# Three Exp/Ln activations and two VectorE steps of a projection stage in another order

## The chip, the cores and the metric

The kernel runs on one core of one Trainium2 chip. The time is the device time of one execution in microseconds; three runs of the kernel before took 3581.80, 3582.93 and 3586.24 us (median 3582.93).

## The reference, cut to what matters

Two blocks of layers run one after the other on 1024 tokens of width 1024. The second block first normalises its input and multiplies it by one wide matrix (w_in, 27 units of 128 output features), and then uses slices of the product in three mixers. The stage of the change computes this product, and beside it the first mixer:

```python
proj = hn @ w_in[l]
(q_sb, k_sb, v_sb, z_ssd, x_ssd, b_ssd, c_ssd, dt_ssd,
 q_hg, f_hg, i_hg, g_hg) = jnp.split(proj, split_at, axis=-1)
...
xbc = jax.nn.silu(causal_depthwise_conv(jnp.concatenate([xs, bm, cm], axis=-1) * vmask, conv_w, conv_b))
...
y = y.reshape(bsz, L, SSD_W) * jax.nn.silu(z.astype(f32))
...
z = jnp.einsum('bhqd,bhkd->bhqk', q[:, :, start:end], k[:, :, :end]).astype(jnp.float32) * scale
log_keep = jnp.where(mask, jax.nn.log_sigmoid(-z), 0.0)
csum = jnp.cumsum(log_keep, axis=-1)
log_w = jax.nn.log_sigmoid(z) + (csum[..., -1:] - csum)
```

The silu of a unit is computed as y * exp(-ln(1 + exp(-y))), with three activations of one table set: Exp, Ln, Exp. The silu lines are the "gates" of the change. The last four lines are the stick-breaking attention, whose cumulative sum is made with matmuls.

## The kernel before, in words

The stage is the function projection_and_sticks. It interleaves two streams of work on all engines.

The first stream is the projection: 27 units u of 128 features, each in three pieces j = 0, 1, 2 of 352, 344 and 344 of the 1040 token columns. A piece has 24 matmuls on TensorE (8 blocks of the contraction, each as three products of upper and lower halves, L155). A unit's weights come in one transfer, are split in an upper half on ScalarE (split_hi, L137) and a lower half on VectorE (split_lo, L142), both issued in piece j = 1 of the unit before. VectorE scales each finished piece out of PSUM (evict, L2996). Units 7 to 14 are the x units: VectorE runs a convolution of four taps over the whole unit (L3072, L3074 at j = 0 of the next unit, L3078 twice at j = 1) and then a max into the tile ce (L3081). Units 15 to 22 are the silu units, with no taps and only the max (L3089). Both kinds are gated: ScalarE runs Exp (L2741), Ln (L2743) and Exp (L2747) over ce in place, VectorE multiplies by it (finish, L3011), and SyncE stores the unit. There is one ce, so the max of a unit waits until finish of the unit before is through (s_out). The semaphores of the gate are s_cm (the max is done), s_cx (the first Exp), s_cl (the Ln), s_ce (the last Exp).

The second stream is the stick-breaking attention: 56 tiles c (14 for each of 4 heads) of up to 512 columns, one tile a slot. For a tile TensorE makes the logits z in one of two banks (L2918, on the diagonal also L2921), ScalarE runs Abs, Exp and Ln (L2767, L2769, L2771), VectorE forms sp (L3112), ScalarE its upper half (L2786) and VectorE its lower half (L3121). TensorE adds the sums to the same bank (L2931, L2933), ScalarE makes the weights from it (L2777), and TensorE multiplies them with the values (L2902). A running sum acc goes along (VectorE L3101, L3103, L3117; ScalarE L2780). Slot c prepares tile c + 1 and finishes tile c.

The order is written out by hand in the function drive, the same for each engine: slot(c), and inside it, at its end, the pieces that fall into the slot. Each engine runs its instructions in that order. Pieces 15 to 59 lie in the slots (2114 to 2440 us of the trace), the rest between the phases of the third mixer's first chunks (sd.act, sd.dve, sd.pe), whose ScalarE instructions L2381, L2384, L2387 and L2391 come at the head of a phase. TensorE waits for L2387 before L2354.

Of the kernel before, what the change touches and what calls it, by code (L numbers as in the profile page):

```python
# [17 lines left out]
ACT = mybir.ActivationFunctionType  # L18
# [2473 lines left out]
def projection_and_sticks(nc, a, w, hi, lo, inv, x, x_again, x_out, over_x, heads, hg, keep, table, cst, proj, conv, o_cat, ident, ones):  # L2492
# [10 lines left out]
    NU = len(units)  # L2503
# [5 lines left out]
    gated = lambda u: is_x(u) or is_silu(u)  # L2509
    n_gated = lambda u: u - 7  # L2510
# [13 lines left out]
    with Stage(nc, "pr") as st:  # L2524
# [17 lines left out]
        ce = st.sb("ce", [P, LM])  # L2542
# [152 lines left out]
        def _(act):  # L2695
# [25 lines left out]
            def piece(p):  # L2721
                u, j = p // 3, p % 3
                if j == 0 and u - 3 in qk:
                    root(u - 3)
                if j == 1 and u + 1 < NU:
                    w.split_hi(act, (u + 1) % 2, (u + 1) // 2, free=(s_mm, 3 * (u - 1) + 3))
                if u - 2 in qk:
                    i = qk.index(u - 2)
                    if j == 0:
                        act.wait_ge(s_ev, 3 * (u - 2) + 3)  # L2730
                        wait(act, s_blk, 3 * i)
                        nc.scalar.activation(ce[:, :], ev[(u - 2) % 3][:, TAPS - 1:], ACT.Square).then_inc(s_psq, 1)
                    c0, c1 = PIECES[j]
                    act.wait_ge(s_blk, 3 * i + j + 1)
                    if j == 0:
                        wait(act, s_nrm, i - 1)
                    nc.scalar.activation(cy[i % 2][:, c0:c1], pb[:, 0:c1 - c0], ACT.Ln, bias=eps[:, :], scale=1.0 / HD).then_inc(s_pb, 1)
                if gated(u - 1) and j == 2:
                    n = n_gated(u - 1)
                    act.wait_ge(s_cm, n + 1)  # L2740
                    nc.scalar.activation(ce[:, :], ce[:, :], ACT.Exp, scale=-1.0).then_inc(s_cx, 1)  # L2741
                    act.wait_ge(s_cx, n + 1)
                    nc.scalar.activation(ce[:, :], ce[:, :], ACT.Ln, bias=1.0).then_inc(s_cl, 1)  # L2743
                if gated(u - 2) and j == 0:
                    n = n_gated(u - 2)
                    act.wait_ge(s_cl, n + 1)
                    nc.scalar.activation(ce[:, :], ce[:, :], ACT.Exp, scale=-1.0).then_inc(s_ce, 1)  # L2747
                if (u, j) == (DT + 2, 0):
                    act.wait_ge(s_sdp, 64)
                    nc.scalar.activation(par[:, 2:3], par[:, 1:2], ACT.Exp).then_inc(s_dte, 1)  # L2750
                    act.wait_ge(s_dt, 2)
                    nc.scalar.activation(tmp, tmp, ACT.Exp, scale=-1.0).then_inc(s_dte, 1)
                    act.wait_ge(s_dte, 2)
                    nc.scalar.activation(tmp, tmp, ACT.Ln, bias=1.0).then_inc(s_dte, 1)
                if (u, j) == (DT + 4, 0):
                    act.wait_ge(s_dtc, 5)
                    for name in ("ecum", "wend", "elast"):
                        nc.scalar.activation(keep[name], keep["cum" if name == "ecum" else name], ACT.Exp).then_inc(s_dtx, 1)

            def slot(c):  # L2760
# [26 lines left out]
                for p in in_slot(c):  # L2787
                    piece(p)
# [162 lines left out]
        def _(dve):  # L2951
# [56 lines left out]
            def finish(u):  # L3008
                dve.wait_ge(s_ce, n_gated(u) + 1)
                src = cy[u % 2][:, :] if is_x(u) else ev[u % 3][:, TAPS - 1:]  # L3010
                nc.vector.tensor_tensor(cy[u % 2][:, :], src, ce[:, :], ALU.mult).then_inc(s_out, 1)  # L3011

            def piece(p):
                u, j = p // 3, p % 3
                if j == 0 and u - 3 in qk:
                    i = qk.index(u - 3)
                    dve.wait_ge(s_scaled, 1)
                    dve.wait_ge(s_r, i + 1)
                    nc.vector.scalar_tensor_tensor((qn, kn)[i % 2][i // 2][:, :], ev[(u - 3) % 3][:, TAPS - 1:], gains[:, i % 2:i % 2 + 1],
                                                   cy[i % 2][:, :], ALU.mult, ALU.mult).then_inc(s_nrm, 1)  # L3020
                    dve.wait_ge(s_nrm, i + 1)
                evict(u, j)
                if j == 1 and u + 1 < NU:
                    w.split_lo(dve, (u + 1) % 2, (u + 1) // 2)
                if (u, j) == (DT + 1, 1):
                    dve.wait_ge(s_kept, 16 * KT)
                    dve.wait_ge(s_sdp, 64)
# [23 lines left out]
                if u - 2 in vs:  # L3051
                    i = vs.index(u - 2)
                    dve.wait_ge(s_vt, 3 * i + j + 1)
                    if i == 0 and j == 0:
                        dve.wait_ge(s_kept, 16 * KT)
                    if j < 2:
                        src = pb[:, :].rearrange("p (t c) -> p t c", c=P)
                        if j == 0:
                            nc.vector.tensor_copy(vt[i][0:META, 0, :], src[0:META, 0, :])
                            nc.vector.tensor_copy(vt[i][:, 1:4, :], src[:, 1:4, :]).then_inc(s_pb, 1)  # L3060
                        else:
                            nc.vector.tensor_copy(vt[i][:, 4:8, :], src).then_inc(s_pb, 1)
                    else:
                        nc.vector.tensor_copy(vt[i][:, 8, :], pb[:, 0:P]).then_inc(s_pb, 1)
                if is_x(u - 1):
                    v, n = u - 1, n_gated(u - 1)
                    src = ev[v % 3]
                    y = cy[v % 2][:, :]
                    if j == 0:
                        wait(dve, s_gone[v % 2], 16 * (n // 2))  # L3070
                        dve.wait_ge(s_ev, 3 * u)
                        nc.vector.tensor_scalar(y, src[:, 0:LM], taps[:, n, 0:1], cbias[:, n:n + 1], ALU.mult, ALU.add).then_inc(s_cc, 1)  # L3072
                        dve.wait_ge(s_cc, 4 * n + 1)
                        nc.vector.scalar_tensor_tensor(y, src[:, 1:1 + LM], taps[:, n, 1:2], y, ALU.mult, ALU.add).then_inc(s_cc, 1)  # L3074
                    if j == 1:
                        for t in (2, 3):
                            dve.wait_ge(s_cc, 4 * n + t)
                            nc.vector.scalar_tensor_tensor(y, src[:, t:t + LM], taps[:, n, t:t + 1], y, ALU.mult, ALU.add).then_inc(s_cc, 1)  # L3078
                        dve.wait_ge(s_cc, 4 * n + 4)
                        wait(dve, s_out, n)  # L3080
                        nc.vector.tensor_scalar(ce[:, :], y, LOWEST, None, ALU.max).then_inc(s_cm, 1)  # L3081
                if j == 0 and gated(u - 2):
                    finish(u - 2)
                if is_silu(u - 1) and j == 1:
                    v, n = u - 1, n_gated(u - 1)
                    wait(dve, s_gone[v % 2], 16 * (n // 2))
# [1063 lines left out]
```

## Time and profile before

| | us |
|---|---|
| profiled execution, its own time | 3581.8 |
| its span | 3580.0 |
| TensorE busy (share of the span) | 3436.8 (96%) |
| VectorE busy | 2168.6 (61%) |
| ScalarE busy | 1538.3 (43%) |
| TensorE's granted clock, mean | 0.983 |

A busy time is the sum over an engine's instructions, overlaps counted once. The granted clock is the mean over the span, as a share of 2.4 GHz. The share of the span says little about one stage; there the table of stretches and the timelines tell more. Busy times of TensorE come from modelled ends, so that its instructions overlap in a timeline.

### The profile page before, as it was taken

What the parts mean: (1) busy time and instruction counts of PE and PEld (TensorE: products, weight loads), DVE (VectorE), ACT (ScalarE), POOL (GpSimd) and SP (SyncE); (2) the same over time, 40 slices, a digit from 0 to 9 for tenths busy, and PEclk for the clock granted to TensorE, in tenths of its full rate; (3) what the DMA queues carried; (4) which work ended last, traced back from release to release, by engine and by line L of the source; (5) the groups of instructions that cost most, each with busy time, mean ns of one, the idle gap of its engine ahead of it and who ended that gap; (6) DMA issues with size and microseconds to landing.
All of it is one profiled execution on the core that took longest, in us unless ns stands there. A gap on an engine that the chain in (4) does not pass through costs nothing. (4 is left out here: it accounts for less than half of the span.)

```text
span 3580.0 us, 48153 instructions
## 1 busy us (share of the span) xinstructions
PE 3436.8 (96%) x17578; PEld 2805.4 (78%) x17578; DVE 2168.6 (61%) x4264; ACT 1538.3 (43%) x3062; POOL 121.8 (3%) x151
## 2 busy tenths in 40 slices
PE   8999999989999999999999899999879999999999
PEld 6878887867777777777777678788867877878887
DVE  5477774475555566666667637766766566644443
ACT  4254453444444454444444436664323322332222
POOL 0000001000000000000000200000000000000000
PEclk9999999999999999999999999999989999999999
DMA  4232225621111221122223411112322222222223
GB/s 148 89 110 96 89 89 175 205 74 57 54 59 56 70 68 60 61 68 71 65 67 108 164 41 35 56 64 85 123 74 94 97 84 78 104 90 98 94 94 124
DMA packets 162585, 316.84 MB, mean 89 GB/s; under 512 B 33744, under 2 KB 79360, under 8 KB 162224
## 3 DMA queue, kind: packets, MB, share of 16 engines
q1 hardware_dynamic: 144432, 268.49, 22.7%
q0 software_dynamic: 15808, 36.89, 3.3%
q10 hardware_dynamic: 2112, 8.39, 0.6%
q8 instruction: 142, 2.33, 0.3%
q14 instruction: 91, 0.75, 0.1%
HBM read 260.22 MB, written 59.71 MB: 89 GB/s over the span
## 5 line engine op out<-in xcount | busy, mean ns | idle before, releaser
L137 ACT ACTIVATE all_w_hi<-all_w_raw 128x1024 fp32r<-128x1024 f32 x241 | 253.5, 1053 | 455.2 <-PE om_z L155 261.2
L142 DVE TENSOR_TENSOR all_w_lo<-all_w_raw,all_w_hi 128x1024 fp32r<-128x1024 f32 x241 | 294.9, 1224 | 244.1 <-ACT all_w_hi L137 243.8
L155 PE MATMUL om_z<-all_hi,all_w_hi 128*128 128x512 f32 x640 | 258.4, 404 | 7.9 <-DVE all_w_lo L142 4.8
L155 PE MATMUL om_z<-all_hi,all_w_lo 128*128 128x512 f32 x640 | 257.1, 402 | 0.0
L155 PE MATMUL om_z<-all_lo,all_w_hi 128*128 128x512 f32 x640 | 254.7, 398 | 0.0
L2122 DVE CUSTOM_DVE_ANT_0 at_logit<-da_qk,at_bias 128x256 f32<-128x256 f32 (+1 forms) x384 | 130.0, 376 | 165.3 <-issue 164.7
L155 PE MATMUL pr_g<-all_hi,all_w_hi 128*128 128x344 f32 (+1 forms) x624 | 213.5, 342 | 11.8 <-PEq L45 4.9
L1668 ACT ACTIVATE at_p<-at_logit,da_pair_max 128x256 f32<-128x256 f32 (+1 forms) x384 | 177.5, 465 | 101.4 <-DVE da_pair_max L2122 101.4
L1660 ACT ACTIVATE at_pt<-da_tr 128x512 f32<-128x512 f32 (+1 forms) x192 | 101.2, 527 | 264.7 <-PE da_tr L1860 264.6
L155 PE MATMUL om_z<-om_h_hi,all_w_hi 128*128 128x512 f32 x512 | 202.4, 395 | 1.7 <-DVE all_w_lo L142 1.7
L155 PE MATMUL pr_g<-all_hi,all_w_lo 128*128 128x344 f32 (+1 forms) x624 | 202.4, 324 | 0.0
L155 PE MATMUL pr_g<-all_lo,all_w_hi 128*128 128x344 f32 (+1 forms) x624 | 201.7, 323 | 0.0
L155 PE MATMUL om_z<-om_h_lo,all_w_hi 128*128 128x512 f32 x512 | 200.0, 391 | 0.0
L155 PE MATMUL om_z<-om_h_hi,all_w_lo 128*128 128x512 f32 x512 | 199.8, 390 | 0.0
L3968 DVE TENSOR_TENSOR all_yo<-all_yo,om_z 128x512 f32<-128x512 f32 x80 | 55.0, 687 | 184.9 <-PE om_z L155 184.8
L1870 PE MATMUL da_pv<-at_v,at_pt 128*128 128x64 f32 x1280 | 164.1, 267 | 0.0
L1870 PEld LDWEIGHTS da_pv<-at_v,at_pt 128*128 128x128 f32 x1280 | 159.8, 192 | 1.9
L2139 DVE TENSOR_TENSOR da_o<-da_pv,da_rden 128x128 f32<-128x128 f32 x192 | 56.0, 292 | 167.4 <-PE da_pv L1870 161.9
L155 PEld LDWEIGHTS om_z<-all_hi,all_w_hi 128*128 128x128 f32 x640 | 122.6, 192 | 37.8 <-DVE all_w_lo L142 5.0
L3863 ACT ACTIVATE om_h_hi<-om_m 128x512 fp32r<-128x512 f32 x64 | 40.5, 632 | 255.2 <-DVE om_m L3966 255.2
L1196 ACT ACTIVATE all_w_hi<-all_w_raw 128x512 fp32r<-128x512 f32 x190 | 118.3, 623 | 72.9 <-PE da_by L1214 23.8
L155 PEld LDWEIGHTS om_z<-all_lo,all_w_hi 128*128 128x128 f32 x640 | 122.8, 192 | 28.2
(827 smaller groups left out, 8882.8 us busy)
## 6 DMA issues: line engine op xcount, KB each, us to landing
all_w_raw<-in_w_mlp SPq DMA_DIRECT2D x128, 512.0 KB, 3.5
all_w_raw<-in_w_qkv SPq DMA_DIRECT2D x136, 256.0 KB, 2.7
all_w_raw<-in_w_ug SPq DMA_DIRECT2D x48, 512.0 KB, 4.1
all_w_raw<-in_w_in SPq DMA_DIRECT2D x27, 512.0 KB, 3.5
all_w_raw<-in_w_v SPq DMA_DIRECT2D x20, 512.0 KB, 4.5
vhat<-ag_vst ACTq DMA_DIRECT2D x4, 2048.0 KB, 7.4
ow_v<-vhat SPq DMA_DIRECT2D x16, 512.0 KB, 3.3
da_before<-o_groups POOLq DMA_DIRECT2D x32, 256.0 KB, 3.8
```

Source lines behind the costliest of these rows:

```text
L137: self.nc.scalar.activation(self.hi[b][:, :], self.raw[b][:, :], ACT.Copy).then_inc(self.hi_done[b], 1)
L142: self.nc.vector.tensor_tensor(self.lo[b][:, :], self.raw[b][:, :], self.hi[b][:, :].bitcast(F32), ALU.subtract).then_inc(self.lo_done[b], 1)
L155: last = self.nc.tensor.matmul(out, wp[b][:, w], ap[:, k, cols], start=(k == 0 and m == 0), stop=(k == KT - 1 and m == 2))
L1196: self.nc.scalar.activation(self.hi[n % self.slots], self.tile[name], ACT.Copy, scale=self.scales[j] if name in ("a11", "a12") else 1.0).t ...
L1660: nc.scalar.activation(pt[t % 2][:, 0:wd], tr[:, 0:wd], ACT.Copy).then_inc(s_pt, 1)
L1668: last = nc.scalar.activation(p[t % 2][:, hh, 0:wd], logit[t % 2][:, hh, 0:wd], ACT.Exp, scale=-1.0, bias=pair_max[:, t, hh:hh + 1], accum ...
L1870: last = nc.tensor.matmul(pv[:, 64 * hh:64 * hh + 64], pt[t % 2][:, i * P:i * P + P], v[:, t + x, 64 * hh:64 * hh + 64], start=(x == 0), s ...
L2122: last = nc.vector.tensor_tensor_reduce(out=logit[t % 2][:, hh, 0:wd], in0=qk[hh][:, 0:wd], in1=bias[ag][hh][x][:, :], scale=1.0, scalar=3 ...
L2139: nc.vector.tensor_tensor(o[:, t, :].rearrange("p (h c) -> p h c", h=2), pv[:, 0:P].rearrange("p (h c) -> p h c", h=2), rden[:, t, :].rear ...
L3863: nc.scalar.activation(h_hi[:, i, :], m[n % 2][:, :], ACT.Square)
L3968: nc.vector.tensor_tensor(x[:, i, halves[h]], x[:, i, halves[h]], z[b][:, :], ALU.add).then_inc(s_ev, 1)
```

## The change

On ScalarE the first Exp of a gate goes from piece j = 2 to piece j = 1 of the following unit, and the last Exp from piece j = 0 of the unit after that to j = 2, right behind the Ln. On VectorE the split of the next unit's weights goes ahead of the eviction at j = 1, and finish goes ahead of the first taps at j = 0. No instruction is added or taken away. TensorE, GpSimd and SyncE keep their order.

```diff
@@ -2735,16 +2735,16 @@
                     if j == 0:
                         wait(act, s_nrm, i - 1)
                     nc.scalar.activation(cy[i % 2][:, c0:c1], pb[:, 0:c1 - c0], ACT.Ln, bias=eps[:, :], scale=1.0 / HD).then_inc(s_pb, 1)
-                if gated(u - 1) and j == 2:
+                if gated(u - 1):
                     n = n_gated(u - 1)
-                    act.wait_ge(s_cm, n + 1)
-                    nc.scalar.activation(ce[:, :], ce[:, :], ACT.Exp, scale=-1.0).then_inc(s_cx, 1)
-                    act.wait_ge(s_cx, n + 1)
-                    nc.scalar.activation(ce[:, :], ce[:, :], ACT.Ln, bias=1.0).then_inc(s_cl, 1)
-                if gated(u - 2) and j == 0:
-                    n = n_gated(u - 2)
-                    act.wait_ge(s_cl, n + 1)
-                    nc.scalar.activation(ce[:, :], ce[:, :], ACT.Exp, scale=-1.0).then_inc(s_ce, 1)
+                    if j == 1:
+                        act.wait_ge(s_cm, n + 1)
+                        nc.scalar.activation(ce[:, :], ce[:, :], ACT.Exp, scale=-1.0).then_inc(s_cx, 1)
+                    if j == 2:
+                        act.wait_ge(s_cx, n + 1)
+                        nc.scalar.activation(ce[:, :], ce[:, :], ACT.Ln, bias=1.0).then_inc(s_cl, 1)
+                        act.wait_ge(s_cl, n + 1)
+                        nc.scalar.activation(ce[:, :], ce[:, :], ACT.Exp, scale=-1.0).then_inc(s_ce, 1)
                 if (u, j) == (DT + 2, 0):
                     act.wait_ge(s_sdp, 64)
                     nc.scalar.activation(par[:, 2:3], par[:, 1:2], ACT.Exp).then_inc(s_dte, 1)
@@ -3012,6 +3012,8 @@
 
             def piece(p):
                 u, j = p // 3, p % 3
+                if j == 1 and u + 1 < NU:
+                    w.split_lo(dve, (u + 1) % 2, (u + 1) // 2)
                 if j == 0 and u - 3 in qk:
                     i = qk.index(u - 3)
                     dve.wait_ge(s_scaled, 1)
@@ -3020,8 +3022,6 @@
                                                    cy[i % 2][:, :], ALU.mult, ALU.mult).then_inc(s_nrm, 1)
                     dve.wait_ge(s_nrm, i + 1)
                 evict(u, j)
-                if j == 1 and u + 1 < NU:
-                    w.split_lo(dve, (u + 1) % 2, (u + 1) // 2)
                 if (u, j) == (DT + 1, 1):
                     dve.wait_ge(s_kept, 16 * KT)
                     dve.wait_ge(s_sdp, 64)
@@ -3062,6 +3062,8 @@
                             nc.vector.tensor_copy(vt[i][:, 4:8, :], src).then_inc(s_pb, 1)
                     else:
                         nc.vector.tensor_copy(vt[i][:, 8, :], pb[:, 0:P]).then_inc(s_pb, 1)
+                if j == 0 and gated(u - 2):
+                    finish(u - 2)
                 if is_x(u - 1):
                     v, n = u - 1, n_gated(u - 1)
                     src = ev[v % 3]
@@ -3079,8 +3081,6 @@
                         dve.wait_ge(s_cc, 4 * n + 4)
                         wait(dve, s_out, n)
                         nc.vector.tensor_scalar(ce[:, :], y, LOWEST, None, ALU.max).then_inc(s_cm, 1)
-                if j == 0 and gated(u - 2):
-                    finish(u - 2)
                 if is_silu(u - 1) and j == 1:
                     v, n = u - 1, n_gated(u - 1)
                     wait(dve, s_gone[v % 2], 16 * (n // 2))
```

The order of the instructions shows it at three places. First ScalarE, from the end of the slot whose piece is j = 1 of an x unit (the one at 2243 us in the trace) on. L2786 is a tile's upper half, L137 the split of the weights, L2792 and L2794 two activations on four columns, L2767 to L2771 the next tile's Abs, Exp and Ln. Before:

```order
L2786 ACTIVATE pr_sp_hi<-pr_sp 128x512
L137 ACTIVATE all_w_hi<-all_w_raw 128x1024
L2792 ACTIVATE pr_oln<-pr_oss,pr_eps 128x4
L2794 ACTIVATE pr_orr<-pr_oln 128x4
L2767 ACTIVATE pr_e<-pr_zb 128x512
L2769 ACTIVATE pr_e<-pr_e 128x512
L2771 ACTIVATE pr_e<-pr_e 128x512
L2777 ACTIVATE pr_wt<-pr_zb 128x512
L2780 ACTIVATE ox_sticks<-pr_acc 128x512
L2786 ACTIVATE pr_sp_hi<-pr_sp 128x512
L2741 ACTIVATE pr_ce<-pr_ce 128x1040
L2743 ACTIVATE pr_ce<-pr_ce 128x1040
```

And in the changed kernel, from the same place:

```order
L2786 ACTIVATE pr_sp_hi<-pr_sp 128x512
L137 ACTIVATE all_w_hi<-all_w_raw 128x1024
L2742 ACTIVATE pr_ce<-pr_ce 128x1040
L2792 ACTIVATE pr_oln<-pr_oss,pr_eps 128x4
L2794 ACTIVATE pr_orr<-pr_oln 128x4
L2767 ACTIVATE pr_e<-pr_zb 128x512
L2769 ACTIVATE pr_e<-pr_e 128x512
L2771 ACTIVATE pr_e<-pr_e 128x512
L2777 ACTIVATE pr_wt<-pr_zb 128x512
L2780 ACTIVATE ox_sticks<-pr_acc 128x512
L2786 ACTIVATE pr_sp_hi<-pr_sp 128x512
L2745 ACTIVATE pr_ce<-pr_ce 128x1040
```

The first Exp of the gate (L2742 in the changed kernel) now stands ahead of the next tile's Abs, Exp and Ln; the Ln (L2745) and the last Exp (L2747) stand behind them.

Second VectorE, at j = 0 of a unit whose two predecessors are gated (L2996 the eviction, L3011 finish, L3074 and L3076 the first taps, L3101 and L3103 the running sum of the next tile):

```order
 L2996 TENSOR_TENSOR pr_ev<-pr_g,all_inv 128x352
-L3072 TENSOR_SCALAR pr_cy<-pr_ev,pr_taps,pr_cbias 128x1040
-L3074 SCALAR_TENSOR_TENSOR pr_cy<-pr_ev,pr_taps,pr_cy 128x1040
 L3011 TENSOR_TENSOR pr_cy<-pr_cy,pr_ce 128x1040
+L3074 TENSOR_SCALAR pr_cy<-pr_ev,pr_taps,pr_cbias 128x1040
+L3076 SCALAR_TENSOR_TENSOR pr_cy<-pr_ev,pr_taps,pr_cy 128x1040
 L3101 COPY pr_acc<-pr_sp 128x128
```

Finish has moved ahead of both taps. At j = 1 the row of L142 has moved from behind the row of L2996 to ahead of it, and all else of the piece stands as it was.

Third ScalarE again, between the phases, at the third gated unit there. L2381 and L2384 are the decay of one chunk, L2387 the copy that TensorE waits for, L2391 the next phase's squares. Before:

```order
L2384 ACTIVATE pr_e<-pr_e 128x512 x2
L137 ACTIVATE all_w_hi<-all_w_raw 128x1024
L2387 ACTIVATE pr_sp<-pr_zb 128x512
L2741 ACTIVATE pr_ce<-pr_ce 128x1040
L2743 ACTIVATE pr_ce<-pr_ce 128x1040
L2747 ACTIVATE pr_ce<-pr_ce 128x1040
```

And in the changed kernel:

```order
L2384 ACTIVATE pr_e<-pr_e 128x512 x2
L137 ACTIVATE all_w_hi<-all_w_raw 128x1024
L2742 ACTIVATE pr_ce<-pr_ce 128x1040
L2387 ACTIVATE pr_sp<-pr_zb 128x512
L2745 ACTIVATE pr_ce<-pr_ce 128x1040
L2747 ACTIVATE pr_ce<-pr_ce 128x1040
```

Here the first Exp has moved ahead of the copy L2387.

## Rows read from the trace of the kernel before

**Rows 1.** Busy table: us, then each engine's busy us (count), clock, DMA, GB/s

```profile
2196.00:2440.00 244.00, 239.61 (x1368) 196.16 (x1367) 179.38 (x308) 165.35 (x302) 1.84 (x2) 1.00 0.16 57
```

**Rows 2.** Waits of PE, 2196 to 2520: total us, times, longest

```profile
PE pr_zb L2931 <- DVE ox_sticks L3121: 4.4, 5, 1.2
...
PE pr_zb L2354 <- ACT pr_sp L2387: 0.7, 1, 0.7
```

**Rows 3.** Timeline of ACT: start, us, engine, line, what [idle before]

```profile
2242.57 1.04 ACT L137 ACTIVATE all_w_hi<-all_w_raw 128x1024 fp32r<-128x1024 f32 x1
...
2244.26 0.60 ACT L2767 ACTIVATE pr_e<-pr_zb 128x512 f32<-128x512 f32 x1 [0.23 <-PE pr_zb L2918]
...
2251.09 1.07 ACT L2743 ACTIVATE pr_ce<-pr_ce 128x1040 f32<-128x1040 f32 x1
...
2252.07 0.58 ACT L2767 ACTIVATE pr_e<-pr_zb 128x512 f32<-128x512 f32 x1
...
2253.35 0.63 ACT L2771 ACTIVATE pr_e<-pr_e 128x512 f32<-128x512 f32 x1
2253.88 0.58 ACT L2777 ACTIVATE pr_wt<-pr_zb 128x512 f32<-128x512 f32 x1
```

**Rows 4.** Timeline of DVE in the same unit

```profile
2243.30 0.51 DVE L2996 TENSOR_TENSOR pr_ev<-pr_g,all_inv 128x344 f32<-128x344 f32 x1
2243.73 1.22 DVE L142 TENSOR_TENSOR all_w_lo<-all_w_raw,all_w_hi 128x1024 fp32r<-128x1024 f32 x1
...
2247.53 0.70 DVE L3081 TENSOR_SCALAR pr_ce<-pr_cy 128x1040 f32<-128x1040 f32 x1
...
2250.15 0.69 DVE L3121 TENSOR_TENSOR ox_sticks<-pr_sp,pr_sp_hi 128x512 fp32r<-128x512 f32 x1
...
2255.62 0.69 DVE L3121 TENSOR_TENSOR ox_sticks<-pr_sp,pr_sp_hi 128x512 fp32r<-128x512 f32 x1
```

**Rows 5.** Timeline of PE in the same unit

```profile
2248.70 1.12 PE L2918 MATMUL pr_zb<-hs_heads 64*128 64x512 f32 x2
2250.89 0.50 PE L2931 MATMUL pr_zb<-ox_sticks,hs_ones 128*128 128x512 f32 x1 [1.06 <-DVE ox_sticks L3121]
```

**Rows 6.** Timelines, first x unit (DVE, PE), then a tile of 256

```profile
2195.61 0.52 DVE L2996 TENSOR_TENSOR pr_ev<-pr_g,all_inv 128x344 f32<-128x344 f32 x1 [2.34 <-PE pr_g L155]
...
2201.82 0.70 DVE L3081 TENSOR_SCALAR pr_ce<-pr_cy 128x1040 f32<-128x1040 f32 x1
...
2203.96 0.33 PE L2931 MATMUL pr_zb<-ox_sticks,hs_ones 128*128 128x128 f32 x1 [0.91 <-DVE ox_sticks L3121]
...
2228.71 0.36 ACT L2767 ACTIVATE pr_e<-pr_zb 128x256 f32<-128x256 f32 x1
...
2229.55 0.42 ACT L2771 ACTIVATE pr_e<-pr_e 128x256 f32<-128x256 f32 x1
...
2230.91 0.42 DVE L3121 TENSOR_TENSOR ox_sticks<-pr_sp,pr_sp_hi 128x256 fp32r<-128x256 f32 x1 [0.25 <-ACT pr_sp_hi L2786]
```

**Rows 7.** Timelines of DVE and PE, first two silu units

```profile
2376.19 0.69 DVE L3089 TENSOR_SCALAR pr_ce<-pr_ev 128x1040 f32<-128x1040 f32 x1
...
2380.30 0.44 PE L2931 MATMUL pr_zb<-ox_sticks,hs_ones 128*128 128x384 f32 x1
...
2396.62 0.69 DVE L3089 TENSOR_SCALAR pr_ce<-pr_ev 128x1040 f32<-128x1040 f32 x1
...
2403.00 0.36 PE L2931 MATMUL pr_zb<-ox_sticks,hs_ones 128*128 128x256 f32 x1
```

**Rows 8.** Timelines of ACT and DVE in the third phase with a gate

```profile
2490.45 0.60 ACT L2387 ACTIVATE pr_sp<-pr_zb 128x512 f32<-128x512 f32 x1 [0.46 <-PE pr_zb L2348]
...
2491.58 0.69 DVE L3089 TENSOR_SCALAR pr_ce<-pr_ev 128x1040 f32<-128x1040 f32 x1
```

**Rows 9.** Timeline of PE, then its stretch: us, busy (count), clock, DMA, GB/s

```profile
2118.39 0.81 PE L2884 MATMUL pr_pb<-pr_ce,mixers_cst 128*128 128x352 f32 x1 [2.25 <-ACT pr_ce L2732]
...
2118.00:2123.00 5.00, 4.61 (x15) 0.66 0.00 0
```

## The prediction, made before the changed kernel was run

> **What bounds the kernel now.** I read the table of stretches first. In the stick slots, 2196 to 2440 us, TensorE is busy 239.6 of 244 us at a granted clock of 1.00 [rows 1]: a stage bound by TensorE, in which a pause of TensorE is lost time and nothing else is. Then TensorE's waits there and in the phases up to 2520: five times, 4.4 us in all, it waited at L2931 for the lower half that VectorE writes at L3121, and once, 0.7 us, at L2354 for ScalarE's copy L2387 [rows 2]. So everything hangs on one chain: z matmul (PE), Abs, Exp, Ln (ACT L2767, L2769, L2771), sp (DVE L3112), upper half (ACT L2786), lower half (DVE L3121), sums (PE L2931). A piece is run between two tiles of this chain, and ScalarE and VectorE run their instructions in the order written.
>
> The timelines show where those waits come from. In an x unit at j = 1, VectorE does the eviction, the split, two taps and the max without a pause: 2243.30 to 2248.23, 4.93 us [rows 4]. The next tile's sp can follow only then; its lower half ends at 2250.84, 2.61 us after the max. TensorE had begun the next z at 2248.70 and was through with it at 2249.82; the sums went on at 2250.89, 1.06 us lost [rows 5]. ScalarE meanwhile had begun the next Abs at 2244.26, long before the max was done [rows 3]: its part of the chain was finished while VectorE worked on the piece.
>
> **The change part by part.** ScalarE's first: the gate's first Exp (L2741 before) moves from piece j = 2 to j = 1. There it waits for s_cm, which VectorE raises with the max at the end of its own piece j = 1, and that piece waits for TensorE's last product of j = 1. Queued behind this wait on ScalarE now stand the next tile's Abs, Exp, Ln, weights, upper halves. Before, they ran beside VectorE's 4.93 us; now they run behind them. Sixteen units have a gate. Twelve of these moves lie in the slots (8 x units, 4 silu units), 4 in the phases.
>
> Full tile (512 columns), from the end C of the max to the end of the lower half. Before 2.61 us. Now: 0.04 to start; the Exp holds ScalarE for 0.98 (L2743 at 2251.09, next Abs at 2252.07); Abs to the end of Ln 1.91 (2252.07 to 2253.98) [rows 3]; end of Ln to the end of the lower half 2.33 (2253.98 to 2256.31) [rows 4]. Together 5.26: 2.65 more. C itself moves too, because the split (L142, 1.22 us) now stands ahead of the eviction: where VectorE sits idle before the eviction it wins up to 1.14 (the split's time less its overlap with the next), where ScalarE's upper half is late it loses. At 2243 the latter: the eviction ran at 2243.30, but L137 ends at 2243.61 [rows 3], so the split, now first, starts at 2243.65 and C is 0.35 later, at 2248.58. And the two small activations L2792 and L2794, which stood in ScalarE's idle time, now stand behind the Exp: another 0.5. That unit costs 3.5 us. The three other full x units, by the same steps, 2.7 to 3.0: together with the first 12.2 us.
>
> Four x units have a narrower next tile. The first (max ends 2202.52) is the cheapest: 2.34 us idle before its eviction, so the whole 1.14 comes back, C at 2201.38; then 0.04 + 0.98, a 256 tile's Abs to Ln 1.26 and 1.36 from there to its lower half, so 2205.0, against 2203.96 where TensorE went on: 1.1 us [rows 6]. With no idle time to win back the same tile costs 2.2. I take 1.1 for this one and 1.5 to 2.3 for the others: 6.7 us for four.
>
> The silu units have no taps. The first has C at 2376.88; plus 5.26 is 2382.14, TensorE went on at 2380.30: 1.8 us. The second has C at 2397.31 and TensorE's need only at 2403.00: even a full tile's 5.26 with 0.4 for the split behind the late upper half ends at 2402.97: nothing [rows 7]. The other two have the same slack (I put them at 0, at most 1 each).
>
> Phases: four moves, three of them before ScalarE work that comes later anyhow. The third is different: in the new order the Exp stands ahead of L2387, which ran at 2490.45 and which TensorE waits for already, 0.7 us [rows 2], while the max ends only at 2492.27 [rows 8]. The copy moves to 2492.27 + 0.04 + 0.98 = 2493.3 and ends at 2493.9 against 2491.05: 2.9 us on TensorE's path.
>
> What the change takes off: the last Exp leaves piece j = 0, 1.06 us of ScalarE x 16, but it was in nobody's way (no wait of TensorE follows it), and the work goes to j = 2, where two activations stand as before. The multiply of finish (L3011) goes ahead of the taps at j = 0: same sum on VectorE, the store a few us earlier, nobody waits for it. Both are 0; if their cover fails, at most 0.5 us x 16 either way. Sum of the direct part: 12.2 + 6.7 + 1.8 + 2.9 = 23.6 us.
>
> Clock. Several of TensorE's pauses grow long, since z has only two banks: the z after next waits until the weights (L2777, 0.48 us past the end of Ln [rows 3]) of the delayed tile are read out. At 2248: max 2248.58, small activations 0.5, Exp 1.02, Abs to Ln 1.91, weights 0.48, so z at 2252.5 and a pause of 3.8 us behind 2248.7. The same steps in the same view give 2.6 at 2268, 3.2 at 2356, 3.5 at 2490, 2.1 at 2201 and 2291. After a 2.25 us pause before 2118.39 the granted clock averaged 0.66 over 2118 to 2123 [rows 9]: with levels of 1.0 (2.4 GHz) and 0.5 (1.2 GHz) that is 3.4 us at the lower one. 15 matmuls ran in those 5 us, where the slots' mean of 1368 in 244 us [rows 1] would have given 26 in the 4.61 busy ones. Half of 3.4 us is 1.7 us of lost work; since in the slots some 0.6 us of such a stretch falls on the second, short pause behind the late z, I take 1.4. The pauses of 1.06 us were followed by none (clock 1.00 throughout rows 1). Of the six long pauses listed, each about as long as that one or longer, I count five with a drop, at 1.4: 7 us. The bounds are 0 and eight drops (every full tile's and long narrow tile's pause, and the phase's) at 1.7, 14 us. The Trainium skill ("TensorE: Matmul & The Clock Gate", section Terms) prices throttled time at one minus the clock ratio, idle or not; by that rule the five drops would be 8.5 us and the sum 1.5 us more. No row here has a drop beside a second pause, so the trace doesn't tell the two apart.
>
> Total 23.6 + 7 = 30.6, say 31 us. The profiled execution took 3581.8 us (span 3580.0), so 3612.8; it lies 1.1 us under the median of the three runs, 3582.9. I predict 3613.5.
>
> **The rivals.** (A) Faster. The split ahead of the eviction uses VectorE's idle time and the first Exp starts sooner, so the five waits at L3121 vanish: 4.4 us less, with 0.7 at L2354 5.1 less, 3577.8. It decides at j = 1 of each x unit, if the max is done before ScalarE could have started the next Abs. For it: 2.34 us idle in rows 6. Against it: in rows 3 and 4 the Abs began 3.97 us before the max ended. The Trainium skill ("Perfetto Trace Analysis", Optimization Strategy) says to take the gaps of the binding engine, find what releases them and make that start sooner; read so, the change is right, and 3577.8 would be its time. The rows show a releaser whose own releaser on ScalarE starts later. (B) The wait is covered: TensorE has enough queued products that only parts over 1 us show, both signs cancel: within 7 us of now, 3583. Against it: before, TensorE already waited in five of these slots, so there is no cover. (C) The direct part alone, no lower clock: 3581.8 + 23.6 = 3605.4, or with fewer narrow tiles hit 3600. (D) All pauses drop the clock and the slower products push the following tile late as well: 23.6 + 14 + 3 = 40.6, 3622.4. (E) The change doesn't do what it says: excluded by the new order of ScalarE's instructions.
>
> **How the numbers follow.** Forecast (five drops) 0.55; C 0.22; D 0.14; B 0.06; A 0.03. The forecast's own range is 3608 to 3618; to leave out no more than two in ten, the range takes in C's centre and most of D: 3601 to 3622. About 0.2% (7 us) is what a measurement of this kernel can tell from no change: faster 0.03, same 0.06, slower 0.91.
>
> **What would show it.** In the new profile TensorE's wait at L2931 for DVE L3121 grows from 4.4 us to about 15, and a new wait of TensorE at L2918 for ScalarE's weights appears (together about 21); L2354 waits 3 to 4 us for L2387. ScalarE's idle time before the gate's first Exp is put down to the max (L3083), 12 times in the slots, 3 to 4 us in an x unit, and the idle time before L2767 mostly goes. The granted clock in the slots falls below 1.00. DVE's idle time before L3112 grows by about 1 to 2 us per x unit. I am wrong if L2767 still starts before the max's end at j = 1; the size is wrong if the pauses are there and the clock stays at 1.00.

## The result and the profile after

The changed kernel took 3624.61 us (median of its timed runs, 3618.87 to 3630.26), the kernel before 3582.36 on the same chip: a ratio of 1.0118, with a 95% interval of 1.0098 to 1.0139. It is 1.2% slower. The forecast was 3613.5 with a range of 3601 to 3622, so the sign and the mechanism were right and the size too small: the median lies 2.6 us above the range. The profiled execution took 3614.36 us (span 3612.6), where 3612.8 had been worked out for it. That this is so close is luck: the stage of the change grew by 34.7 us where 30.6 were forecast, with two errors of opposite sign in the sum, and the rest of the kernel was 2.1 us shorter than in the profile before.

TensorE's waits between 2190 and 2570 us (who waits, for whom: us in total, times, longest):

```profile
PE pr_zb L2918 <- ACT pr_wt L2777: 17.4, 9, 3.7
PE pr_zb L2931 <- DVE ox_sticks L3121: 4.6, 6, 1.5
PE pr_zb L2354 <- ACT pr_sp L2387: 3.5, 1, 3.5
PE pr_ob L2342 <- DVE ox_ab L2409: 2.7, 2, 2.2
PE pr_pb L2372 <- DVE pr_wt L2442: 0.2, 1, 0.2
```

Against [rows 2] the wait at L2931 stayed, that at L2354 grew by 2.8 us, and 17.4 us at L2918 are new: TensorE waits for a bank of logits that ScalarE has not read out yet.

The table of stretches, first the stretch of [rows 1], then six short ones inside it and one in the phases (busy us and count of PE, PEld, DVE, ACT, POOL, then the granted clock, the DMA share and GB/s):

```profile
2196.00:2440.00 244.00, 222.07 (x1184) 181.72 (x1184) 156.97 (x273) 140.62 (x265) 1.84 (x2) 0.93 0.14 49
2204.00:2211.00 7.00, 7.00 (x27) 6.57 (x26) 4.35 (x12) 4.50 (x8) 0.00 (x0) 0.53 0.01 2
2259.00:2266.00 7.00, 7.00 (x22) 5.11 (x23) 5.07 (x10) 6.21 (x10) 0.00 (x0) 0.56 0.30 89
2280.00:2287.00 7.00, 4.33 (x24) 2.95 (x23) 3.64 (x6) 6.69 (x13) 0.00 (x0) 1.00 0.01 2
2310.00:2314.00 4.00, 4.00 (x20) 4.00 (x19) 2.69 (x7) 3.90 (x9) 0.00 (x0) 0.63 0.02 4
2361.00:2368.00 7.00, 6.73 (x23) 5.57 (x23) 4.00 (x7) 5.48 (x9) 0.00 (x0) 0.53 0.00 0
2385.00:2392.00 7.00, 6.57 (x24) 4.90 (x25) 1.61 (x5) 3.34 (x6) 0.00 (x0) 0.54 0.01 2
2525.00:2529.00 4.00, 4.00 (x18) 4.00 (x18) 2.12 (x4) 0.83 (x1) 0.00 (x0) 0.63 0.00 0
```

Where [rows 1] had TensorE busy for 239.6 us in 244, there are 222.1, and the 1.00 of the clock has become 0.93. The short stretches show where: behind a pause the clock lies near 0.5, its lower level of 1.2 GHz, for some 7 us or some 3.4 us. The fourth row (2280) is a pause of 1.85 us with no drop behind it.

One x unit from close up, the one of [rows 3 to 5]. ScalarE, then VectorE, then TensorE (start, us, what, and in brackets the idle time before and who ended it):

```profile
2249.06 1.04 ACT L137 ACTIVATE all_w_hi<-all_w_raw 128x1024 fp32r<-128x1024 f32 x1
2255.10 1.07 ACT L2742 ACTIVATE pr_ce<-pr_ce 128x1040 f32<-128x1040 f32 x1 [5.00 <-DVE pr_ce L3083]
2256.07 0.28 ACT L2792 ACTIVATE pr_oln<-pr_oss,pr_eps 128x4 f32<-128x4 f32 x1
2256.39 0.21 ACT L2794 ACTIVATE pr_orr<-pr_oln 128x4 f32<-128x4 f32 x1
2256.50 0.58 ACT L2767 ACTIVATE pr_e<-pr_zb 128x512 f32<-128x512 f32 x1
...
2258.30 0.58 ACT L2777 ACTIVATE pr_wt<-pr_zb 128x512 f32<-128x512 f32 x1
```

```profile
2254.36 0.70 DVE L3083 TENSOR_SCALAR pr_ce<-pr_cy 128x1040 f32<-128x1040 f32 x1
```

```profile
2254.94 0.32 PE L155 MATMUL pr_g<-all_lo,all_w_hi 128*128 128x352 f32 x1
2258.94 2.07 PE L2918 MATMUL pr_zb<-hs_heads 64*128 64x512 f32 x2 [3.67 <-ACT pr_wt L2777]
2260.94 0.79 PE L2931 MATMUL pr_zb<-ox_sticks,hs_ones 128*128 128x512 f32 x1
```

And the lower half that L2931 needs (VectorE):

```profile
2260.04 0.69 DVE L3121 TENSOR_TENSOR ox_sticks<-pr_sp,pr_sp_hi 128x512 fp32r<-128x512 f32 x1
```

Before, the next tile's Abs (L2767) began 0.65 us after the split's end [rows 3]. Now it stands behind an Exp that waits 5.00 us for VectorE's max. Abs, Exp, Ln and the weights follow at 2256.50 to 2258.88, and only then can TensorE start its next z at 2258.94: 3.67 us idle. That z then takes 2.07 us, where [rows 5] had 1.12: the clock has fallen. The steps of the prediction are all there to see; it had 3.8 us for this pause. ScalarE's idle time before the first Exp is longer than it had, though, 5.5 us in the mean of the eight x units and not 3 to 4:

```profile
L2742 ACT ACTIVATE pr_ce<-pr_ce 128x1040 f32<-128x1040 f32 x10 | 10.7, 1073 | 49.3 <-DVE pr_ce L3083 43.9 <-DVE pr_ce L3089 5.4
```

### The profile page after: what moved, and what is told of

The parts are those of the page before. It is cut to its first block and busy times, and to the rows that moved or that the text cites. A ratio compares the mean times of both kernels' runs of the same rounds, so it can differ in the third digit from the quotient of the medians.

```text
span 3612.6 us, 48153 instructions
## 1 busy us (share of the span) xinstructions
PE 3451.5 (96%) x17578; PEld 2817.6 (78%) x17578; DVE 2170.2 (60%) x4264; ACT 1537.2 (43%) x3062; POOL 121.9 (3%) x151
## 5 line engine op out<-in xcount | busy, mean ns | idle before, releaser
L142 DVE TENSOR_TENSOR all_w_lo<-all_w_raw,all_w_hi 128x1024 fp32r<-128x1024 f32 x241 | 295.1, 1225 | 256.8 <-ACT all_w_hi L137 256.8
L137 ACT ACTIVATE all_w_hi<-all_w_raw 128x1024 fp32r<-128x1024 f32 x241 | 253.5, 1053 | 454.8 <-PE om_z L155 261.5
```

The source lines that it names most:

```text
L137: self.nc.scalar.activation(self.hi[b][:, :], self.raw[b][:, :], ACT.Copy).then_inc(self.hi_done[b], 1)
L142: self.nc.vector.tensor_tensor(self.lo[b][:, :], self.raw[b][:, :], self.hi[b][:, :].bitcast(F32), ALU.subtract).then_inc(self.lo_done[b], 1)
```

## The experiments

For each profiled run the stage was measured in the same way: from the first z matmul (2106.9 us in the kernel before) to the first matmul behind the stage (2569.5), 462.6 us before; the sum of TensorE's waits on the stage's tiles inside it (13.5 before); and the time inside it at the lower clock level, from the trace's record of the clock (10.6 before). All differences are to these. The table has every run; the last column is what is left of the length when the waits are taken off, divided by the added time at the lower level.

| kernel | ratio, timed runs | stage length | waits | low clock | (length − waits) / low |
|---|---|---|---|---|---|
| changed | 1.0118 | +34.7 | +19.3 | +34.3 | 0.45 |
| changed, again | 1.0112 | +34.6 | +19.2 | +34.3 | 0.45 |
| e1 ScalarE's part | 1.0113 | +42.7 | +20.5 | +52.5 | 0.42 |
| e2 VectorE's part | 1.0003 | −1.1 | −0.8 | −0.7 | |
| e3 three at j = 2 | 1.0008 | +5.9 | +1.1 | +12.3 | 0.39 |
| e5 x units | 1.0074 | +30.1 | +14.9 | +33.3 | 0.46 |
| e6 silu units | 1.0032 | +11.1 | +4.6 | +14.1 | 0.46 |
| e7 split at j = 2 | 1.0101 | +43.4 | +20.3 | +49.7 | 0.46 |
| e10 three at j = 1 | 1.0187 | +73.6 | +41.2 | +78.2 | 0.41 |
| e4 filler | 1.0093 | +31.9 | +9.8 | +21.1 | |
| e11 more filler | 1.0090 | +27.5 | +2.8 | +6.9 | |
| e9 tap at j = 2 | 0.9982 | −3.8 | −3.5 | −0.5 | |

The diffs in this section are shortened: repeated lines and arguments are left out, and "Exp", "Ln", "wait s_cm", "max" or "tap t" stands for the line that does it.

**Which part of the change costs.** The first kernel is the kernel before with ScalarE's edit alone, the second the kernel before with VectorE's two edits alone (the diffs are the two halves of the change).

> ScalarE's part of the change alone; VectorE in the order of before. Theory 1 (ScalarE waits for the max ahead of the next tile's Abs, so that TensorE pauses, and the pauses bring lower clocks): the whole loss is here, 3618 to 3635 us, TensorE waiting 16 to 19 us at L2918 for the weights. Theory 2 (VectorE's new order, above all the split that waits for ScalarE's upper half ahead of the eviction, makes the loss): 3580 to 3590 us.

Measured: 3622.01 against 3585.64 us, 1.0113 (1.0093 to 1.0133). The waits at L2918 were 17.7 us, nine times.

> VectorE's part alone (split ahead of the eviction, finish ahead of the taps); ScalarE in the order of before. Theory 1: no loss, 3576 to 3586 us, TensorE's wait at L2931 for L3121 3 to 5 us as before (4.4). Theory 2: most of the loss, 3605 us or more. Since finish now stands ahead of the taps while the last Exp still runs at j = 0, VectorE may wait for ScalarE there; a wait of more than 1 us each would show as 5 to 10 us more.

Measured: 3586.71 us, 1.0003 (0.9994 to 1.0012). The whole loss is ScalarE's; VectorE's part alone is worth nothing that the times can tell. Beside ScalarE's part it does move single pauses, by about what the prediction gave: with ScalarE's part alone the first x unit's pause is 3.23 us and with both 2.10 (it had 1.14 won back), and that of the unit at 2248 is 3.33 and 3.67 (it had 0.35 lost). In the profiles the stage is 8 us shorter with both; 18 us less at the lower clock level go with that, and the timed runs do not show the difference.

**Which of the three activations.** The changed kernel, with the first Exp put back to j = 2 and the last left there:

```diff
-                if gated(u - 1):
-                    if j == 1: wait s_cm; Exp
-                    if j == 2: wait s_cx; Ln; wait s_cl; Exp
+                if gated(u - 1) and j == 2:
+                    wait s_cm; Exp; wait s_cx; Ln; wait s_cl; Exp
```

> The changed kernel with the first Exp back at j = 2, so that all three activations of the gate stand there, 3.2 us in a row. Theory 1: the loss is gone, 3578 to 3590 us; at most a small pause of TensorE where the slot after j = 2 has less than 1 us of slack (at most 8 times 0.5 us). Theory 2: 3605 us or more, as VectorE's order is the changed one. Rival to both (three activations in a row block as much as a wait does): 3600 us.

Measured: 3586.8 us, 1.0008 (0.9999 to 1.0017). Moving the last Exp costs at most this, 6 us at the upper end of the interval; the first Exp's place, ahead of the next tile's Abs, is the cause. Together with the first kernel that leaves one instruction, 16 times.

**Where.** First Exp at j = 1 only for the x units, then only for the silu units:

```diff
-                    if j == 1:
+                    if j == (1 if is_x(u - 1) else 2):
                         act.wait_ge(s_cm, n + 1)
```

> The changed kernel, with the first Exp at j = 1 only for the 8 x units; for the silu units it stands at j = 2 as before. Theory: the cost is TensorE's pauses behind the delayed tile plus the work lost at the lower clock. In the changed kernel the x units held 14.6 us of waits at L2918 and most of the 4.6 at L2931, and 24 of the 37.5 us at the lower clock (half of them, 12, lost); so this kernel should lie 23 to 29 us above the kernel before. Rival 1 (nearly all comes from the phase and from the silu units, whose pauses come late): under 12 us. Rival 2 (the pauses alone cost, and the clock lies at the lower level anyway): 15 us.

Measured: 3611.35 against 3585.14 us, 1.0074 (1.0058 to 1.009), 26 us. Waits at L2918: 16.5 us, eight times. The expectation had put one x unit's pause (1.98 us at 2381) down to a silu unit; the time lay within its bounds.

> The mirror image: the first Exp at j = 1 only for the 8 silu units (4 in the slots, 4 between the phases), and at j = 2 for the x units. Theory: one pause of 2 us in the first silu unit, 2.8 us more at L2354, and two or three stretches of 3.4 us at the lower clock: 7 to 12 us above the kernel before, and the sum of this difference and that of the x units alone equals that of the whole change within 5 us. Rival (a pause in one unit makes the next ones worse, so that the two parts are not additive): the two together fall short of the whole by 10 us or more.

Measured: 3597.89 us against 3585.14, 1.0032 (1.0021 to 1.0042), 11 us by the ratio. Of it, 2.8 us are the wait at L2354, which has the forecast length to the tenth (3.5 us, once), and 1.4 new waits at L2918. 0.74 and 0.32% make 1.06, the whole 1.12: the parts add up.

**Is it the pauses that bring the clock down?** TensorE was kept busy through the delay, with dummy products behind each x unit's j = 1 (28 in all), and then with more of them and in the silu units of the slots too (48 in all; the diff is of this second kernel):

```diff
+                for p in in_slot(c):
+                    if p % 3 == 1 and gated(p // 3 - 1):
+                        pe.wait_ge(s_ev, p)
+                        for _ in range((4, 3, 7, 5, 4, 3, 4, 6, 5, 3, 2, 2)[n_gated(p // 3 - 1)]):
+                            nc.tensor.matmul(g[0][:, 0:2 * P], ident, ...)
```

> The changed kernel, with 28 matmuls on constants (128x256, about 0.5 us each) that nobody reads, put on TensorE behind piece j = 1 of the eight x units, where it pauses: 2 to 6 of them a pause, about 14.7 us in all, less than the pauses themselves. They compute nothing of the output. Clock theory (some 15 us of the profiled run's loss and 25 us of the median's is TensorE at its lower clock level behind the pauses): clock in the slots 0.98 or more, time 3600 to 3608 us, less spread between runs. Rival (the pauses alone make the loss, the clock comes along at no cost): 3620 us or more. If the filler is too long for the pauses it adds at most 5 us.

Measured: 3617.85 against 3585.64 us, 1.0093 (1.0076 to 1.011), 4.2 us under ScalarE's part alone on the same chip; time at the lower level in the stage 31.8 us instead of the changed kernel's 44.9. The time lies above the 3600 to 3608 that the clock theory had, and the intervals of the two ratios overlap: too little to decide. Pauses of up to 1.5 us stayed in the slots, and 3.5 us at L2354.

> The changed kernel with dummy products (128x256, one more behind each x unit's j = 1 than in the filler kernel before it, and 2 to 5 behind the four silu units' too), so that TensorE is busy through the delay instead of idle. Left-out work: none; the dummy products' results aren't used. Theory: the stretches at the lower clock between 2196 and 2440 us, 34 us in the changed kernel, fall to under 10, which gives back 12 us, while the dummy products cost up to 6 us where they are longer than the pause: 6 to 12 us under the changed kernel. Rival (the lower clock doesn't come from the pauses): the low stretches stay, and the kernel is no faster or up to 6 us slower than the changed one.

Measured: 3617.64 against 3584.82 us, 1.009 (1.0076 to 1.0104). The stretch of [rows 1] in it:

```profile
2196.00:2440.00 244.00, 238.32 (x1326) 196.80 (x1325) 163.70 (x283) 145.67 (x273) 1.84 (x2) 0.99 0.15 51
```

The clock is back at 0.99 and TensorE busy 238 us (dummy products counted). The delay itself is unchanged: ScalarE waits 49.3 us ahead of the ten first Exps between 2196 and 2440, as in the changed kernel. Only what TensorE does meanwhile differs, so the lower clock came from the idle time. The time at the lower level in the stage fell from 44.9 to 17.5 us (in the slots one stretch of 6.8 us is left, under the 10 expected) and the stage's length by 7.2 us. That is within the 6 to 12 expected; at 0.45 us each the 27.4 us less at the lower level are worth 12, so the dummy products cost about 5. In the timed runs the gain is 8 to 10 us by the ratios, but the intervals (1.0076 to 1.0104 against 1.0098 to 1.0139 and 1.0094 to 1.013) overlap: the profiles show the clock's part, the times only agree with it.

**Does the loss grow with the delay?** The changed kernel with all three activations at j = 1, so that each gate holds ScalarE 2.1 us longer:

```diff
-                    if j == 2:
+                    if j == 1:
                         act.wait_ge(s_cx, n + 1)
```

> The changed kernel with all three activations of a gate at j = 1, so that each of the 12 gates in the slots and the one ahead of L2387 hold ScalarE 2.1 us longer (Ln 1.07, Exp 1.04). Theory: each of the 8 pauses in x units, the first silu unit's and the phase's grow by about 2.1 us and two silu units get one: TensorE's waits at L2918, L2931 and L2354 grow from 25 to 45 to 50 us, and the whole loss keeps its ratio to them (40 over 20 in the changed kernel, 35 over 20 where the weight split was moved), so 70 to 90 us above the kernel before. Rival (a stretch at the lower clock follows a pause once, whatever the pause's length): the pauses grow by 22 and the clock's part stays at 14 to 20, so 60 us above before.

Measured: 3650.21 against 3584.82 us, 1.0187 (1.0174 to 1.0201), 65 us. TensorE's waits, and two stretches behind pauses:

```profile
PE pr_zb L2916 <- ACT pr_wt L2775: 39.8, 11, 5.9
PE pr_zb L2354 <- ACT pr_sp L2387: 5.7, 1, 5.7
...
PE pr_zb L2929 <- DVE ox_sticks L3119: 1.5, 3, 0.7
```

```profile
2196.00:2440.00 244.00, 208.53 (x1044) 170.72 (x1043) 142.06 (x239) 122.36 (x223) 1.84 (x2) 0.87 0.12 42
2238.00:2249.00 11.00, 9.59 (x33) 8.48 (x34) 2.79 (x11) 3.95 (x15) 0.00 (x0) 0.53 0.00 0
2269.00:2280.00 11.00, 9.00 (x28) 7.11 (x29) 5.75 (x10) 6.41 (x12) 0.00 (x0) 0.53 0.20 60
```

The waits grew as expected (47 us at the three lines). The timed runs lie between the two expectations, nearer to the rival's 60. In the profile, which was the slowest of the four runs, the stage is 73.6 us longer, of which 41.2 are waits and 32.4 the clock. So in the profile the rival, whose clock part stays at 14 to 20 us, is wrong. With longer pauses there were longer stretches (10.2 us four times here, none above 6.8 in the changed kernel), and the clock's part grew from 15 to 32 us, in step with the waits. Single pauses don't follow it: 10.2 us stand with one of 3.6 us, 6.8 with one of 5.7 and 3.4 with one of 3.8.

**Another wait, the same loss.** An attempt to make VectorE's piece j = 1 shorter in the kernel before:

```diff
-                evict(u, j)
-                if j == 1 and u + 1 < NU:
+                if j == 2 and u + 1 < NU:
                     w.split_lo(dve, (u + 1) % 2, (u + 1) // 2)
+                evict(u, j)
```

> The kernel before, with the VectorE half of the weight split (L142) moved from piece j = 1 to j = 2, ahead of the eviction there; nothing else is changed. Theory: VectorE's piece j = 1 of an x unit becomes 1.2 us shorter, so the five waits of TensorE at L2931 for L3121 (4.4 us in all) go: 3 to 5 us faster than before. Rival: j = 2 then carries the split into a tile that was on time, or the next unit's first product waits for the split: no change, or up to 3 us slower, with a new wait at L155 or the waits at L2931 moved to j = 2.

Measured: 3620.16 against 3585.14 us, 1.0101 (1.0083 to 1.0119). The waits:

```profile
PE pr_g L155 <- DVE all_w_lo L142: 20.3, 10, 4.4
...
PE pr_zb L2354 <- ACT pr_sp L2387: 0.7, 1, 0.7
PE pr_zb L2931 <- DVE ox_sticks L3121: 0.4, 1, 0.4
```

This kernel is slower, where the theory had it 3 to 5 us faster. The waits at L2931 went, as the theory had it, and the rival's came (25.8 us over the whole stage), many times larger than it was priced: TensorE begins the next unit in the slot in which it ends j = 2, while VectorE is still at the tile of that slot. It was useful all the same. This kernel has none of the changed kernel's new waits, and with 20 us more of waits of another kind its stage has 50 us more at the lower clock, about as much as ScalarE's part alone, and the changed kernel's ratio in the last column of the table.

**A kernel with a shorter stage.** In the kernel before, of an x unit the fourth tap and the max go to j = 2, the first Exp and the Ln to j = 0 of the unit after, the last Exp and finish to j = 1 there (the diff has VectorE's part):

```diff
-                    if j == 1:
-                        for t in (2, 3): tap t
+                    if j > 0: tap j + 1
+                    if j == 2:
                         max
-                if j == 0 and gated(u - 2): finish(u - 2)
+                if gated(u - 2) and j == (1 if is_x(u - 2) else 0): finish(u - 2)
```

> The kernel before, with VectorE's longest piece made shorter: of an x unit the fourth tap and the max go from j = 1 to j = 2, the gate's first Exp and Ln to j = 0 of the unit after, its last Exp and finish to j = 1 there. The silu units keep their places. VectorE's piece j = 1 falls from 4.9 to 4.1 us (eviction, split, one tap, finish), j = 0 from about 4 to 2.9, j = 2 grows to 2.4; no ScalarE instruction waits for a max made in the same piece. Theory: most of the waits at L2931 (4.4 us in five) go, so 2 to 5 us faster than before. Rival: 0.8 us less at j = 1 clears only half of them and ScalarE's two more at j = 0 (2.1 us) make new ones: within 2 us of before.

Measured: 3576.16 us (nine runs) against 3584.82 (thirteen), 0.9982 (0.9972 to 0.9992). Its wait at L2931, and VectorE's piece at j = 1 in the unit of [rows 4]:

```profile
PE pr_zb L2931 <- DVE ox_sticks L3122: 0.8, 2, 0.4
```

```profile
2243.81 0.51 DVE L2996 TENSOR_TENSOR pr_ev<-pr_g,all_inv 128x344 f32<-128x344 f32 x1
2244.23 1.22 DVE L142 TENSOR_TENSOR all_w_lo<-all_w_raw,all_w_hi 128x1024 fp32r<-128x1024 f32 x1
2245.37 1.29 DVE L3078 SCALAR_TENSOR_TENSOR pr_cy<-pr_ev,pr_taps,pr_cy 128x1040 f32<-128x1040 f32 x1
2246.58 1.23 DVE L3011 TENSOR_TENSOR pr_cy<-pr_cy,pr_ce 128x1040 f32<-128x1040 f32 x1
```

The piece lasts 4.0 us (2243.81 to 2247.81) instead of 4.93, the wait of 4.4 us fell to 0.8, and the stage is 3.8 us shorter. The interval of the timed runs excludes no change, but the medians lie 8.7 us apart where the stage gives 3.8, and 0.18% is no more than the 0.2% that the prediction gave as what a measurement of this kernel can tell: the shorter stage is shown, the faster kernel is likely. The profiled execution itself took 3583.62 us: outside the stage it had 20.9 us more at the lower level than that of before, so it shows the mechanism and not the gain. It was timed on one chip only.

**The changed kernel a second time,** for the spread of its times.

> The changed kernel once more, unchanged, for a second profile and more times. Theory: its pauses are the same to 1 us (17 us at L2918, 4 to 5 at L2931, 3.5 at L2354), and what makes its runs differ by 16 us is how many of the pauses the lower clock follows: time against the mean granted clock lies on one line, about 3.6 us for 0.001 of clock. Rival: the pauses themselves differ from run to run by 5 us or more.

Measured: 3621.11 against 3585.14 us, 1.0112 (1.0094 to 1.013). In the second profile (3619.59 us) not only the waits are the same (17.4, 4.5 and 3.5 us); so are the seven stretches at the lower level in the slots and phases, one by one, in place and length. The expectation that it varies behind which pauses the clock falls is wrong for this pair. The 5 us between the two profiles lie outside the stage, 2.0 ahead of it and 3.3 behind it, where the second has 6.7 us more at the lower level. The first set of timed runs does follow the mean clock (0.977, 0.975, 0.975, 0.973 for 3618.87, 3622.37, 3626.86, 3630.26 us), but a timed run leaves no trace, and so where in the kernel it lost the clock is open.

## Why the prediction was too small

Bound and chain: right. TensorE's pauses are the loss, and they come from one instruction's place on ScalarE, as the first three experiments show.

The direct part was 23.6 us; the waits grew by 19.3. The large terms hold: the pause of the unit at 2248 was put at 3.8 us and is 3.67, that of the first x unit 2.1 and 2.10, that at 2291 2.1 and 2.07, L2354's wait 2.9 longer and it is 2.8. By the growth of the waits the silu units came to 1.9 us for 1.8. The 4 us that were too many are the x units': 18.9 us forecast, 14.8 measured (the waits ahead of z and of the sums, less those of before). The pauses expected at 2268 (2.6) and 2356 (3.2) came to 1.85 and 1.98. In the unit at 2248 the waits grew by 2.6 us and not by 3.5, though its pause had nearly the forecast length: its z took 2.07 us at the lower clock, to 2261.01, and VectorE's lower half was ready at 2260.73; a z of 1.12 us would have ended at 2260.06 and left a second wait of some 0.7. The slower clock hides a part of the direct loss. The prediction also expected the wait at L2931 to grow to 15 us and that at L2918 to make up the rest of 21; together they are 22.0, but 17.4 of it at L2918. Its own paragraph on the clock had put five pauses, 13.8 us, ahead of a z, so this sign did not follow from its steps. The bank that TensorE needs next is read out late, so TensorE stops ahead of z, and by the end of z the lower half is there or nearly so (0.82 us were left at 2284, 0.87 at 2385).

The failed step is the clock's: "I count five with a drop, at 1.4: 7 us." The stage lost 15.4 us to it (34.7 less 19.3). The cost of a microsecond at the lower level was right: 1.4 for 3.4 us is 0.41, and the table has 0.39 to 0.46. Wrong was how long the clock stays down. The five drops of 3.4 us are 17 us; measured were 34.3 more: from 2190 to 2570 us stand seven stretches, 37.5 us in all, of which four last 6.8 us (before, in the same work, one of 3.4 at 2456). The 3.4 us came from a single example [rows 9], and the trace of before holds longer ones that I did not read. Two of its stretches:

```profile
2455.00:2462.00 7.00, 5.16 (x28) 5.19 (x29) 3.77 (x9) 1.57 (x3) 0.00 (x0) 0.76 0.36 122
2566.00:2573.00 7.00, 3.47 (x32) 3.31 (x32) 0.33 (x2) 1.25 (x3) 0.00 (x0) 0.54 0.80 247
```

The first is a drop of 3.4 us, the second, at 0.54 over all its 7 us, one of 6.8. But that one stands at an idle time longer than any the change makes:

```profile
PE hg_sc L3355 <- PEq L45: 8.2, 1, 8.2
```

All six stretches of 6.8 us in the trace of before stand at pauses of 4.3 us or more. Its pauses of 1.7 to 3.4 us brought 3.4 us (twelve times) or none (eight times), and once, with a second pause close behind, 10.2. So reading them all would have widened the bound but not moved the centre much; that pauses of 1.87 to 3.67 us brought 6.8 us four times is what the changed kernel showed, and why is open. Priced with both lengths, five drops would have been 7 to 14 us, and eight, the bound taken, up to 27: rival D should have reached 3635, and the range with it.

The Trainium skill ("TensorE: Matmul & The Clock Gate", section Terms) prices throttled time at one minus the clock ratio, here a half, and sets no idle time in it apart. Half of 34.3 is 17.2, and 19.3 + 17.2 = 36.5, against 34.7 measured. A price under a half, as the prediction had it, is borne out: 0.39 to 0.46 in every profile without dummy products whose stage grew. That pauses inside the low stretches are the reason fits the traces (the pause that ends at 2258.94 overlaps its stretch) but was not tested.

The other part of the miss is in the timed runs. Their median lies 10 us above the profiled execution and 42.2 above before; the second set gave 36.0. Counted with the profiled execution, as the second set and the one before are, the first set's median is 3622.37, 40.0 above before. The stage explains 34.7 of each; the rest goes with the mean clock and has no place in a trace. Taking a profiled execution's sum to the median with 1 us added was too narrow for a kernel that runs at a varying clock.

Rival A fell with VectorE's part alone: with the split ahead of the eviction and ScalarE's order as before, the waits at L2931 were 4.9 us in four. B fell as well. C (3605.4) lacked the clock. D had the sum nearest, 3622.4, and its 14 us for the clock are close to the 15.4, but by luck in part: it had eight drops of 3.4 us where there were seven, four of them twice as long, a direct part 4.3 us too large, and 3 us for tiles pushed late that no run separates. The 0.14 given to it was too little.

## What to carry to other kernels

Before an instruction that waits for another engine is moved up in an in-order queue, list what then stands behind it and who feeds on that; a slack that nobody waited for is cheaper than an earlier start. On a kernel bound by TensorE, multiply each new microsecond of pause: here it cost 1.8 to 2.4 in the end (the stage's length over its waits, in the kernels whose waits grew by 4 us or more and had no dummy products). Small pauses count too: with all three activations at j = 2 the waits grew by 1.1 us only, yet with pauses of 1.2 to 1.6 us the stage had 12.3 us more at the lower clock and was 5.9 us longer. And take the length of a lower-clock stretch from all of those in the trace, not from one, with the longest as the bound.

## What the hardware showed that was not expected

In the stage, behind a pause, the lower level lasted 3.4, 6.8 or 10.2 us, and once, where the split was moved, 13.7. It did not follow every pause: in the changed kernel none came behind 1.85 us at 2280 and 1.62 at 2332, one of 6.8 us came behind 1.87 at 2358, and one of 3.4 behind 3.51 us at 2520. What decides this is open. In the stage two profiles of the changed kernel have the same stretches at the same places. Elsewhere they don't: behind the same pause of 3.38 us at 1930, well ahead of the stage, the first was at the lower level for 6.8 us and the second for 3.4 (0.83 and 0.91 of granted clock over these 20 us, first profile, then second):

```profile
1925.00:1945.00 20.00, 16.62 (x62) 12.98 (x61) 8.98 (x14) 8.38 (x14) 0.00 (x0) 0.83 0.19 62
1925.00:1945.00 20.00, 16.62 (x65) 13.08 (x64) 10.47 (x18) 10.29 (x16) 0.00 (x0) 0.91 0.29 104
```

So the same order of instructions can give either length. Filled pauses kept the clock up: 0.99 over the slots with dummy products, 0.93 without, at the same delay on ScalarE.
